# Gate and up tiles of a SwiGLU FFN multiplied as 2x2 blocks with seven block products in place of eight

## The reference, cut to what matters

```
h2  = rmsnorm(x, g_norm2) * (1 + scale2) + shift2
ffn = (silu(h2 @ w_ffn_gate) * (h2 @ w_ffn_up)) @ w_ffn_down
x   = x + gate2 * ffn
```

## Time and profile before

| | |
|---|---|
| median of three runs | 1994.87 us |
| the profiled execution | 1995.31 us |
| its span, from first to last instruction | 1993.4 us |
| mean granted PE clock | 0.986 of full |
| PE, DVE, ACT, POOL busy | 98%, 41%, 31%, 30% |
| chain that ended last | PE 88%; DVE 6%; issue 2% |
| matmuls of `tile3` (L1819) in that chain | 24% of the span |
| matmuls of "down" (L1928) in that chain | 13% of the span |

### The profile page before, as it was taken

How to read it: one execution, slowest core, us unless ns; L and a number is a source line. 1 busy time by engine, 2 the same in 40 slices (tenths; PEclk the granted TensorE clock), 3 DMA queues, 4 the chain that set the end, 5 groups by cost and what they waited for, 6 DMA issues and landing times.

```text
span 1993.4 us, 30848 instructions
## 1 busy us (share of the span) xinstructions
PE 1943.9 (98%) x12749; PEld 1859.1 (93%) x12749; DVE 822.3 (41%) x1460; ACT 611.8 (31%) x1276; POOL 595.0 (30%) x506
## 2 busy tenths in 40 slices
PE   7899999999999999999989999999999999999997
PEld 4899999999999999999988999999999999999997
DVE  5730463403644136441264676134134324323336
ACT  4523334233343333433324544111111111111113
POOL 3212232211422123321131864323322322332330
PEclk8999999999999999999998999999999999999998
DMA  9241221422214222133241642111111111111112
GB/s 337 63 107 43 74 73 50 135 54 72 75 54 131 53 77 75 49 107 82 67 129 49 217 130 64 52 45 43 48 48 43 52 45 43 51 45 43 49 47 88
DMA packets 211251, 154.91 MB, mean 78 GB/s; under 512 B 10196, under 2 KB 195732, under 8 KB 210600
## 3 DMA queue, kind: packets, MB, share of 16 engines
q1 hardware_dynamic: 210810, 152.73, 26.2%
q10 hardware_dynamic: 302, 0.22, 0.0%
HBM read 131.42 MB, written 21.50 MB: 77 GB/s over the span
## 4 chain that ended last, share of the span: by engine, by line
PE 88%; DVE 6%; issue 2%; POOL 2%; ACT 1%; DMA 1%; DVEq 0%; ACTq 0%; SPq 0%; POOLq 0%
PE bank L913 35%; PE bank L1819 24%; PE bank L1928 13%; PE bank L998 3%; PE bank L1852 2%; PE bank L1016 1%; PE bank L1018 1%; PE bank L1021 1%; PE bank L949 1%; PE bank L1059 1%; DMA w_ada_ring<-in_w_ada 1%; POOL mix L1306 1%; DVE y_rows L2219 1%; PE bank L936 1%; DVE y_rows L2276 1%
## 5 line engine op out<-in xcount | busy, mean ns | idle before, releaser
L1259 POOL TENSOR_TENSOR w_lo<-w_raw,w_hi 128x512 fp32r<-128x512 f32 x128 | 180.5, 1411 | 710.8 <-ACT w_hi L1081 710.8
L913 PE MATMUL bank<-h_hi,w_hi 128*128 128x352 f32 x1536 | 331.7, 338 | 1.6 <-ACT w_hi L1081 1.6
L913 PE MATMUL bank<-h_hi,w_lo 128*128 128x352 f32 x1536 | 312.2, 325 | 1.2 <-POOL w_lo L1259 1.1
L913 PE MATMUL bank<-h_lo,w_hi 128*128 128x352 f32 x1536 | 311.4, 325 | 0.0
L913 PEld LDWEIGHTS bank<-h_hi,w_hi 128*128 128x128 f32 x1536 | 253.9, 190 | 23.3 <-issue 18.5
L913 PEld LDWEIGHTS bank<-h_hi,w_lo 128*128 128x128 f32 x1536 | 259.1, 189 | 2.7 <-POOL w_lo L1259 2.7
L913 PEld LDWEIGHTS bank<-h_lo,w_hi 128*128 128x128 f32 x1536 | 259.7, 189 | 0.0
L2085 POOL TENSOR_TENSOR f_lo<-w_raw,f_hi 128x512 fp32r<-128x512 f32 x88 | 116.7, 1349 | 291.4 <-ACT f_hi L1964 291.4
L2253 DVE SCALAR_TENSOR_TENSOR x_t<-bank,ada,x_t 128x352 f32<-128x352 f32 (+1 forms) x288 | 164.1, 570 | 56.6 <-PE bank L1928 37.1
L2085 POOL TENSOR_TENSOR w_lo<-w_raw,w_hi 128x512 fp32r<-128x512 f32 x88 | 117.0, 1350 | 100.6 <-ACT w_hi L1964 100.6
L2199 DVE SCALAR_TENSOR_TENSOR early<-early,bank 128x352 f32<-128x352 f32 x66 | 34.5, 522 | 219.6 <-ACT early L2013 219.6
(11 more groups left out here) (393 smaller groups left out, 3477.5 us busy)
## 6 DMA issues: line engine op xcount, KB each, us to landing
w_raw<-in_w_in SPq DMA_DIRECT2D x128, 256.0 KB, 3.0
w_ada_tile<-in_w_ada SPq DMA_DIRECT2D x32, 512.0 KB, 4.4
w_raw<-in_w_out SPq DMA_DIRECT2D x48, 256.0 KB, 2.8
w_raw<-in_w_ffn_gate SPq DMA_DIRECT2D x44, 256.0 KB, 3.0
w_raw<-in_w_ffn_up SPq DMA_DIRECT2D x44, 256.0 KB, 3.0
w_raw<-in_w_ffn_down SPq DMA_DIRECT2D x44, 256.0 KB, 2.7
w_ada_ring<-in_w_ada SPq DMA_DIRECT2D x8, 1024.0 KB, 7.5
x_scratch<-x_turned_rows SPq DMA_DIRECT2D x1, 4224.0 KB, 13.8
```

The lines of the kernel that those rows point to most:

```text
L913: last = pe.matmul(g.ps[b][:, 0:n], x[:, s, k, :], y[:, 4 * h + k, c0:c0 + n], start=(h == 0 and k == 0 and m == 0), stop=(h == 1 and k == ...
L1259: pool.tensor_tensor(Wl[:, s], raw[:, r], Wh[:, s].bitcast(F32), ALU.subtract).then_inc(s_lo, 1)
```

## The change

The first three tile pairs stay as they were ("plain"), now one step each. For the other 19 ("seven") the pair is taken as a product of 2x2 blocks: the gate tile's weights are A11 (rows k 0 to 3) and A12 (k 4 to 7), the up tile's A21 and A22; h2 is B11, B12 (k 0 to 3, columns 0 to 527 and 528 to 1055) and B21, B22 (k 4 to 7). Seven products of one weight word and one block of h2 take the place of eight: A11 B11, S2 T2, S1 T1, S3 T3, A12 B21, S4 B22, A22 T4, with S1 = A21+A22, S2 = S1-A11, S3 = A11-A21, S4 = A12-S2 and T1 = B12-B11, T2 = B22-T1, T3 = B22-B12, T4 = T2-B21. Each product is 24 matmuls of 264 columns (two pieces by 3 by 4), so a pair takes 168.

The T blocks are made once: DVE forms 16 chunks of 128x528 with 44 instructions, ACT copies each high part, and DVE (`t_lo`) subtracts it for the low part, 16 more. This is spread over the plain steps, the first "down" and the first seven. T4 takes B12's place. The S words are made for each seven by DVE with 4 instructions of 128x512 (`combine_first`, `combine_second`, `combine_third`), in the raw slots and one more buffer; then ACT and POOL split 7 words for a pair where they split 4 halves before. The transfers stay 4 a pair.

The results are put together on DVE: 14 instructions on 264 columns that add or subtract a bank, and 8 with both tensor operands in SBUF; ACT makes 2 copies of the first product, 4 tanh and 4 high parts, POOL 4 low parts, all of 264 columns. Eight banks are used.

`ORDER` now runs pair, pair, "down" of these same two pairs. "down" first multiplies the first activation tile into six pieces, and only then waits for the second tile. Small buffers move into space that the mixer has left, the wait for `eps` goes, and the transfer of the final gain now waits for the last low activation.

```diff
-        ORDER = [("out", s) for s in range(NPC * KC)] + [("proj", 0)]
-        for j in range(LOOP):
-            ORDER += [("proj", 2 * j + 1), ("down", 2 * j), ("proj", 2 * j + 2), ("down", 2 * j + 1)]
-        ORDER.append(("down", NBLK - 1))
+        RAWS = {"out": 2, "plain": 4, "seven": 4, "down": 4}
+        HALVES = {"out": 2, "plain": 4, "seven": 7, "down": 4}
+        PIECES = {"out": 1, "plain": 6, "seven": 14, "down": 24}
...
+        unit = lambda f: ("plain" if f < NPLAIN else "seven", f)
+        ORDER = [("out", s) for s in range(NPC * KC)]
+        for j in range(NBLK):
+            ORDER += [unit(2 * j), unit(2 * j + 1), ("down", j)]
...
+        BANKS, freed, n = {}, [0] * 8, 0
+        for step in ORDER:
+            if step[0] == "seven":
+                banks = [0, 1, 2, 3, 4, 5, 6, 7, 0, 1, 2, 3, 6, 7]
+            elif step == ("down", 0):
+                banks = ([(n + TURN + k) % 4 for k in range(4)] + [4, 5, 6, 7]) * 3
+            elif step[0] == "down":
+                banks = [4, 5, 0, 1, 2, 3, 6, 7] * 3
+            else:
+                banks = [(n + TURN + k) % 4 for k in range(PIECES[step[0]])]
+                n += PIECES[step[0]]
+            BANKS[step] = []
...
+        PRODUCTS = (("A11", "B11"), ("S2", "T2"), ("S1", "T1"), ("S3", "T3"), ("A12", "B21"), ("S4", "B22"), ("A22", "T4"))
+        WORD = [w for w, _ in PRODUCTS]
+        P1, P6, P5, P7, P2, P3, P4 = range(7)
+        AT_RAW = {"A11": 0, "S2": 0, "A21": 1, "S3": 1, "A22": 2, "A12": 3, "S4": 3}
+        COMBINED = {"S1": 1, "S3": 2, "S2": 3, "S4": 4}
...
-                return src[:, 4 * h:4 * h + 4, bass.ds(b * (2 * P) + (t // 2) * P, P)]
+            if kind != "down":
+                t, h = (k // 2, k % 2) if kind == "plain" else ((0, 0), (1, 0), (1, 1), (0, 1))[k]
+                return (w_gate, w_up)[t][:, 4 * h:4 * h + 4, b * P:(b + 1) * P]
...
+        T_AT = {(0, 1): (0, 1), (1, 0): (2, 3, 4, 5), (1, 1): (6, 7, 8), (2, 0): (10, 11)}
...
-                    s, turns, before = pl.half(k)
-                    wait(sp, s_lo, before - (RING - 1))
+                    s, _, n = pl.raw(k)
+                    if n >= RING:
+                        lows, combined = RELEASE[n - RING]
+                        sp.wait_ge(s_lo, lows)
+                        wait(sp, s_comb, combined)
                     sp.dma_start(raw[:, s], source(kind, b, k)).then_inc(s_w[s], 16)
...
-                            c0, w = span(c)
-                            for f in range(2):
-                                for m, (x, y) in enumerate(((Wh, Ah), (Wh, Al), (Wl, Ah))):
-                                    last = pe.matmul(g.ps[bnk][:, 0:w], x(sl[f])[:, n, :], y[:, par, f, c0:c0 + w],
-                                                     start=(f == 0 and m == 0), stop=(f == 1 and m == 2))
-                            if r == 11:
-                                last.then_inc(s_used, 2)
-                            else:
-                                last.then_inc(s_piece, 1)
+                        s, _, before = pl.half(2 * nh + f)
+                        pe.wait_ge(s_lo, before + 1)
+                        c0, w = span(r % 3)
+                        for m, (x, y) in enumerate(((Wh, Ah), (Wh, Al), (Wl, Ah))):
+                            last = pe.matmul(g.ps[bnk][:, 0:w], x(s)[:, r // 3, :], y[:, f, c0:c0 + w],
+                                             start=(f == 0 and m == 0), stop=(f == 1 and m == 2))
+                        if f and r == 11:
+                            last.then_inc(s_used, 2)
+                        elif f:
+                            last.then_inc(s_piece, 1)
+                    if nh == 0:
+                        pe.wait_ge(s_al, acts(2 * b + 1))
+                        for r in range(6):
+                            half_piece(r, 0)
+                        pe.wait_ge(s_al, acts(2 * b + 2))
+                        for r in range(6):
+                            half_piece(r, 1)
+                    for r in range(0 if nh else 6, 12):
+                        half_piece(r, 0)
+                        half_piece(r, 1)
...
+            def seven(f, pl):
+
+                for p, (word, block) in enumerate(PRODUCTS):
+                    s, _, n = pl.half(p)
+                    pe.wait_ge(s_hi, n + 1)
+                    if nth(f) == 0 and block[0] == "T":
+                        pe.wait_ge(s_tfl, len(FORMED) - FORMED[::-1].index((block, 3)))
+                    for q in range(2):
+                        bnk, turns = pl.piece(2 * p + q)
+                        wait(pe, s_pf[bnk], turns)
+                        for m, (x, y) in enumerate(((Wh, 0), (Wh, 1), (Wl, 0))):
+                            if q == 0 and m == 2:
+                                pe.wait_ge(s_lo, n + 1)
+                            for kk in range(4):
+                                last = pe.matmul(g.ps[bnk][:, 0:HQ], x(s)[:, kk, :], BLOCK[block][kk][y][:, q * HQ:(q + 1) * HQ],
+                                                 start=(m == 0 and kk == 0), stop=(m == 2 and kk == 3))
+                        last.then_inc(s_used if q else s_pr, 1)
...
+                s, _, n = pl.half(k)
+                word, place, combined = SOURCE[n]
+                if word in COMBINED:
+                    act.wait_ge(s_comb, combined + COMBINED[word])
+                else:
+                    act.wait_ge(s_w[place[0]], place[1] * 16 + 16)
+                wait(act, s_used, n - (RING - 1))
+                act.activation(Wh(s), made_of(n), ACT.Copy).then_inc(s_hi, 1)
...
+                def ready(p, q):
+                    bnk, turns = pl.piece(2 * p + q)
+                    act.wait_ge(s_pf[bnk], turns + 1)
+                if FORMER[("seven", f)][0] != "seven":
+                    hi(pl, 2)
+                hi(pl, 3)
+                if nth(f) == 0:
+                    t_hi(12, 13)
+                for q in range(2):
+                    wait_product(act, pl, P1, q)
+                    if nth(f):
+                        act.wait_ge(s_ac, 4 * nth(f))
+                    else:
+                        act.wait_ge(s_al, acts(f))
+                    bnk, _ = pl.piece(2 * P1 + q)
+                    act.activation(P1C[q], g.ps[bnk][:, 0:HQ], ACT.Copy).then_inc(s_pf[bnk], 1)
+                hi(pl, 4)
+                if nth(f) == 0:
+                    t_hi(14, 15)
+                for k in (5, 6, 7):
+                    hi(pl, k)
+                for q in range(2):
+                    ready(P2, q)
+                    act.activation(THQ[q], P1C[q], ACT.Tanh, scale=0.5).then_inc(s_th, 1)
+                hi(pl, 8)
+                for q in range(2):
+                    ready(P3, q)
+                    act.wait_ge(s_sg, 2 * nth(f) + q + 1)
+                    act.activation(THQ[q], U3[q], ACT.Tanh, scale=0.5).then_inc(s_th, 1)
+                hi(pl, 9)
+                for j in range(4):
+                    c0 = (2 + j) % 4 * HQ
+                    act.wait_ge(s_ac, 4 * nth(f) + j + 1)
+                    act.activation(Ah[:, f % NACT, c0:c0 + HQ], (U3 if j < 2 else SG1)[j % 2], ACT.Copy).then_inc(s_ah, 1)
+
             def gate_piece(pl, f, c):
-                wait_full(act, "proj", pl, 6 * f + c)
...
+                elif kind == "seven":
+                    if FORMER[(kind, b)][0] != "seven":
+                        lo(pl, 2)
+                    for k in range(3, 10):
+                        lo(pl, k)
+                    for j in range(4):
+                        c0 = (2 + j) % 4 * HQ
+                        pool.wait_ge(s_ah, acts(b) + j + 1)
+                        pool.tensor_tensor(Al[:, b % NACT, c0:c0 + HQ], (U3 if j < 2 else SG1)[j % 2],
+                                           Ah[:, b % NACT, c0:c0 + HQ].bitcast(F32), ALU.subtract).then_inc(s_al, 1)
...
-                    ahead(lo, pl, 1)
-                    if not is_last(b):
+                    if FORMER[(kind, b)][0] == "plain":
+                        lo(pl, 2)
+                    lo(pl, 3)
+                    if b < NBLK - 1:
                         ahead(lo, pl, 2)
...
+                        if k == 10 and b == 0:
+                            form(9)
+                        if k == 6 and FOLLOWING.get((kind, b), ("", 0))[0] == "seven":
+                            combine_first(FOLLOWING[(kind, b)][1])
+                        if k == 16 and FOLLOWING.get((kind, b), ("", 0))[0] == "seven":
+                            combine_second(FOLLOWING[(kind, b)][1])
...
+            def form(*which):
+
+                for e in which:
+                    name, k = FORMED[e]
+                    t = t_temp(e)
+                    of = lambda n: BLOCK[n][k]
...
+                    wait(dve, s_tf, e)
+                    if name == "T1":
+                        link(sub_(t, of("B12")[0].bitcast(F32), of("B11")[0].bitcast(F32)))
+                        link(dve.tensor_tensor(t, t, of("B12")[1].bitcast(F32), ALU.add))
```

(88 more changed lines are left out.)

374 lines of the change are left out of this document (246 added, 128 removed).

## The result

The changed kernel takes 1975.8 us (median of 4 runs, 1972.8 to 1976.2), the kernel before beside it 1994.9; the ratio is 0.990, 95% interval 0.988 to 0.992. The forecast was 1978. The profiled execution took 1975.96 us, its span is 1974.2, its mean granted clock 0.983.

What follows compares the result with a forecast made beforehand. The prediction took the FFN to be bound by PE's matmuls: 1995.3 - 48.3 (sevens) + 13.5 (waits at "down") + 18 (T blocks) = 1978.5, with the median 0.4 lower, so 1978 us; range 1948 to 2002.

Steps and rivals of the forecast that it cites:

- The pace of 264 columns: In the sevens: 122 ns a matmul, between constant overhead (123.3) and proportional (120.0); 19 sevens save 48.3 us.
- The wait at "down": In each of nine regular blocks PE waits 1.5 us for POOL's last activation low parts; 13.5 us in all.
- The T blocks: Making them on DVE delays work PE waits for, in four places; together 21, taken as 18 us.
- (a): Plain 0: two T chunks and POOL's `lo` delay the multiplication that frees the next tile's bank; 4.3 us.
- (b): Plain 1: T instructions and POOL's between them free the first gate bank late; 3.7 us.
- (c): Second half of plain 1: T instructions make low parts late for the first "down"; 3.5 us.
- (d): First seven: T instructions stand ahead of S4, 6 us late, and the end is late at "down" 1 by 3.7.
- rival D: The change works as said but PE's clock falls in the new waits; up to 5 us more, inside the range.
- (A): Rival: PE stays bound by its matmuls, chains hidden but for 0.3 us a block and 8 once; 1957 us; chance 0.28.
- (B): Rival: the lock between DVE and POOL makes DVE the bound; 24 us slower, 2018 us; chance 0.14.
- a mean near 0.9: Sign: DVE's two-input instructions take 0.43 or up to 1.5 us, with this mean.
- (C): Rival: the weight load doesn't hide behind 110 ns; break-even 137 ns, at 140 the time is 2035 us; chance 0.08.

Runs made afterwards that it cites:

- e4: Changed kernel with two of the three products of every half in a seven streaming 200 of their 264 columns; 1953.2 us (one run).
- e6: Changed kernel with a weight half's split deferred before "down", S4 copied earlier, and T chunks moved from plain 0, three into the first "down"; 1959.5 us.
- e5: Changed kernel with ACT copying the high part of S4 ahead of the last two T4 chunks in the first seven; 1976.5 us (one run).
- e11: The changed kernel again, unaltered; its profiled run took 1969.2 us, the other three 1975.5 to 1976.8.
- e2: Changed kernel with a buffer of 4 bytes a partition ahead of the raw weights, no instruction changed; 1963.4 us, ratio to before 0.984.
- e8: The kernel of e6 with 4 bytes of padding ahead of the raw weight buffers; 1951.8 us, ratio to before 0.979.

## Why the prediction came out right

**The pace of 264 columns** (taken 122, ends 115.3 and 160): 122.05 in the regular blocks. The step held: the pace is 12 ns over the columns, between the constant 13.3 and the proportion 10, and e4 puts the floor under it at 112.5, near the 115 of the earlier trace rows.

The Trainium skill (TensorE: Matmul & The Clock Gate, "Back-to-back issue gap") gives columns/2.4 + about 2.5 ns as the gap of an isolated matmul, 112.5 here, and says that in a stream of weight loads and matmuls both set the spacing; the trace has 122. The prediction used the formula for such a stream, and the Trainium skill does not.

**The wait at "down"** (taken 1.5, ends 0.1 and 3.0): 0.76. The place is as forecast, and so is what ends it, POOL's activation low parts behind the low part of a weight half. The term was sized by POOL and DVE taking turns, 0.71 + 0.35 us for each subtraction. Around these four subtractions, in order of time, first POOL, then DVE:

```profile
1536.35 1.29 POOL L2272 TENSOR_TENSOR w_lo<-w_raw,w_hi 128x512 fp32r<-128x512 f32 x1 [1.63 <-ACT w_hi L2100]
1537.60 3.46 POOL L2306 TENSOR_TENSOR act_lo<-ffn_temps,act_hi 128x264 fp32r<-128x264 f32 x4
...
1536.48 1.44 DVE L2537 SCALAR_TENSOR_TENSOR ffn_temps<-ffn_temps 128x264 f32<-128x264 f32 x1
...
1538.30 0.53 DVE L2543 SCALAR_TENSOR_TENSOR ffn_temps<-ffn_temps 128x264 f32<-128x264 f32 x1
```

Four take 3.46 without a gap, 0.865 each and not 1.06, and nearly all the difference (4 x 0.195 = 0.78) is the difference in the wait. Only one of DVE's instructions there is held up for long (1.44 against 0.43), by the weight half's subtraction; the two behind it take 0.53 and 0.54. This made the sum 6.7 us too high.

**The T blocks** (taken 18, ends 8 and 26): 17.4, near by offsetting errors, which is luck. The waits themselves came to 11.1, not 18: (a) plain 0 3.9 (4.3 forecast); (b) plain 1 nothing in place of 3.7; (c) 0.5, 0.7 and 0.7 in place of 3.5; (d) 2.8 and 2.5 in place of 6 and 3.7. The clock made up for most of it: it fell at (a) and at the "down" behind the first seven, 2.9 + 1.7 us. Some 0.7 are plain matmuls at 162.2 ns in place of 160, and the last 1.0 is not assigned. The prediction had that as rival D (up to 5 us) and left it out of the sum. e6 confirms both for (a): the wait and the fall went together. The first wait of (d), ended by ACT's copy of S4, is there as forecast with 2.8 in place of 6; e5 shows what the term leaves out, that DVE is late for the next product as well, so that the copy alone is worth nothing.

**Costed at nothing:** words and weights. No row of waits names any of them in the regular blocks; these steps held. The layout was costed at nothing as well ("the small buffers"), and here the prediction failed: 4.5 us ahead of the FFN between the two profiled executions, by the spacing of loads (162.0 against 160.9 ns) and falls of the clock (in e11's profile, with fewer falls, the same kernel reaches the landmark at 1224.1, and nothing is lost), and 12.4 us against the same program with its buffers 32 bytes further. Had the buffers fallen as in e2, the kernel would have been at 1963, still in the range, and the forecast of 1978 too high by 15.

**The sum.** 1995.3 - 48.2 + 6.8 + 17.4 + 4.5 = 1975.8, where the profiled execution took 1976.0. The wait at "down" was taken 6.7 us too high and the layout 4.5 too low. So the mechanism in the FFN is the one forecast, and that the total comes within 2 us is in part luck.

**The rivals.** (A), all hidden at 1957, did not come: the waits are there. With the order of work mended (e6, 1959.5) the change comes near it, and with the buffers moved as well (e8, 1951.8) under it. (B), DVE as the bound, did not come. DVE by line (busy us, mean ns, idle before):

```profile
L2536 DVE SCALAR_TENSOR_TENSOR ffn_temps<-ffn_temps 128x264 f32<-128x264 f32 x38 | 30.9, 812 | 1.5 <-ACT ffn_temps L2194 1.5
...
L2529 DVE SCALAR_TENSOR_TENSOR ffn_temps<-ffn_temps 128x264 f32<-128x264 f32 x38 | 15.7, 436 | 1.5 <-ACT ffn_temps L2189 0.2
```

The worst line with two inputs in SBUF has a mean of 812 ns, 0.38 over the 0.43 of an undisturbed one, and L2529 loses nothing; (B) needed a mean loss of 0.88 over all 24. The four such lines on 264 columns (these two, L2537 with 788 and L2543 with 508) have a mean of 0.64 us, so the sign "a mean near 0.9" did not come either: the two engines met less often than assumed. (C), the weight load not hidden, is refuted by 122 ns.
